# Expert-choice lists in three parts by token range, built partly between the tiles of the output projection

## The reference, cut to what matters

```python
def expert_choice_ffn(h, w_router, w_gate, w_up, w_down):
    t = h.reshape(bsz * n, d)
    cap = max(1, EC_CAPACITY * t.shape[0] // N_EXPERTS)     # 128 of 1024 latents, 32 of 256 context tokens
    aff = jax.nn.softmax((t @ w_router).astype(jnp.float32), axis=-1)
    top_w, top_i = lax.top_k(aff.T, cap)
    xe = t[top_i]
    ...
    out = jnp.zeros_like(t).at[top_i.reshape(-1)].add(ye.reshape(-1, d))
```

## Time and profile before

| | us |
|---|---|
| median of 3 runs | 4786.63 (4785.16 to 4791.69) |
| span of the profiled execution (first to last instruction) | 4782.1 |
| PE busy, share of the span | 4300.4 (90%) |
| VectorE busy, share of the span | 1126.3 (24%) |
| tile loop of the first layer | from 1163.95 to 1340.31 |
| lists of the first layer, from the copy of the rows to the last copy of the merge | from 1341.48 to 1382.22 |

### The profile page before, as it was taken

The page is one execution under the profiler, slowest core; times in us unless marked ns, Lnnn a source line. Parts: engine busy times, 40 slices in busy tenths (PEclk is TensorE's granted clock), DMA queues, the critical chain, the costliest instruction groups (busy, mean ns, idle before and its releaser), DMA issues. The chain is left out here.

```text
span 4782.1 us, 61479 instructions
## 1 busy us (share of the span) xinstructions
PE 4300.4 (90%) x25695; PEld 3548.2 (74%) x25695; DVE 1126.3 (24%) x2316; ACT 1134.9 (24%) x2317; POOL 1134.7 (24%) x1008
## 2 busy tenths in 40 slices
PE   7999999999949999999979998989997699999996
PEld 4677686845549989999967685867454699999996
DVE  2333334411240000001033344333013200001102
ACT  2333333301311111111133333332013111111112
POOL 0605244100112222122214426060001112222221
PEclk7999999999969999999969999999998899999998
DMA  6101111013237667776431111010143467676665
GB/s 228 50 16 40 29 32 38 20 35 132 100 113 242 227 223 242 237 241 232 138 83 36 34 28 50 6 50 6 45 161 123 140 234 239 230 235 223 221 227 183
DMA packets 402928, 618.65 MB, mean 129 GB/s; under 512 B 15110, under 2 KB 167916, under 8 KB 402508
## 3 DMA queue, kind: packets, MB, share of 16 engines
q1 hardware_dynamic: 389980, 571.09, 34.9%
q0 software_dynamic: 12672, 43.26, 3.9%
HBM read 561.88 MB, written 53.48 MB: 129 GB/s over the span
## 5 line engine op out<-in xcount | busy, mean ns | idle before, releaser
L895 PE MATMUL ps<-area,ring 128*128 128x160 f32 x8192 | 1166.1, 306 | 109.2 <-DMA ring<-in_w_up_dram 109.2
L895 PEld LDWEIGHTS ps<-area,ring 128*128 128x128 f32 x8192 | 1151.4, 195 | 122.2 <-issue 120.9
L559 PE MATMUL ps<-ring 128*128 128x512 f32 (+1 forms) x1920 | 715.5, 534 | 50.0 <-issue 26.4
L559 PEld LDWEIGHTS ps<-ring 128*128 128x128 f32 x1920 | 370.3, 195 | 386.8 <-issue 371.3
L522 PE MATMUL ps<-cst,area 128*128 128x128 f32 (+2 forms) x2748 | 402.0, 287 | 236.3 <-DVE area L1423 77.1
L928 PE MATMUL ps<-area,ring 128*128 128x160 f32 x4096 | 597.2, 300 | 0.0
L928 PEld LDWEIGHTS ps<-area,ring 128*128 128x128 f32 x4096 | 562.8, 190 | 4.3
L522 PEld LDWEIGHTS ps<-cst,area 128*128 128x128 f32 (+2 forms) x2748 | 319.9, 147 | 299.1 <-issue 81.8
L1502 POOL TENSOR_TENSOR ring<-ring,condT 128x1024 f32<-128x1024 f32 x128 | 258.4, 2018 | 631.3 <-DMA ring<-in_w_ada_dram 616.3
L1567 POOL DMA_INDIRECT xres<-area,curi x64 | 95.4, 1491 | 1270.7 <-DVE area L1465 1261.0
L1459 DVE TENSOR_TENSOR area<-ps,area 128x160 f32<-128x160 f32 x256 | 83.1, 325 | 1165.7 <-ACT area L1128 1165.7
(11 more groups left out here) (232 smaller groups left out, 4320.8 us busy)
## 6 DMA issues: line engine op xcount, KB each, us to landing
ring<-in_w_gate_dram SPq DMA_DIRECT2D x64, 2048.0 KB, 8.5
ring<-in_w_up_dram SPq DMA_DIRECT2D x64, 2048.0 KB, 14.0
ring<-in_w_down_dram SPq DMA_DIRECT2D x64, 2048.0 KB, 10.1
ring<-in_w_ada_dram SPq DMA_DIRECT2D x64, 512.0 KB, 3.8
area<-xres SPq DMA_DIRECT2D x50, 512.0 KB, 4.1
ring<-in_w_in_dram SPq DMA_DIRECT2D x48, 512.0 KB, 6.1
area<-in_w_ada_dram SPq DMA_DIRECT2D x32, 512.0 KB, 15.0
xres<-area SPq DMA_DIRECT2D x28, 512.0 KB, 2.7
```

The lines of the kernel that those rows point to most:

```text
L559: last = mm(dst[:, a:b], hw[:, j, k, :], hT[:, k, a:b], start=(k == 0), stop=(k == KT - 1))
L895: last = mm(ps[:, at:at + CAP], slot(2 * half + i)[:, k, P * (m % 4):P * (m % 4) + P], xeT[b][:, k, :], start=(k == 0), stop=(k == KT - 1))
```

## The change

The 48 rows are no longer worked together. They become three parts on 16 partitions each: part 0 is the latents of tiles 0 to 3, part 1 those of tiles 4 to 7, part 2 the 256 context tokens. PE turns a part to rows as soon as its affinities exist (`aff_rows`): part 0 in pass 6, part 1 in pass 10, part 2 after pass 11. On VectorE, part 0's 16 rounds stand at the ends of passes 6 to 9, four in each; part 1's rows are taken at the end of pass 10 with 5 rounds, its other 11 rounds follow pass 11, and part 2's 4 rounds, on rows of 256, follow these. The preparation of a padded tile and of the parts' first tokens goes. At the end PE turns six small pieces back instead of two, and VectorE copies them out in two instructions instead of one. The merge is the same.

```diff
+                def aff_rows(part):
+                    pe.wait_ge(aff_ready, (4, 8, T)[part])
+                    if part:
+                        pe.wait_ge(rows_copied, part)
+                    for j in range(PARTS[part] // P):
+                        last = transposes(ps[0:EXPERTS, 7 * BANK + P * j:7 * BANK + P * j + P], affs[:, part, j])
+                    last.then_inc(aff_rows_ps, 1)
...
+                    if i == 6:
+                        aff_rows(0)
+                    if i == T:
+                        aff_rows(1)
+                aff_rows(2)
                 pe.wait_ge(lists_ready, 1)
-                for i, src in enumerate((tv, tf)):
-                    last = transposes(ps[:, LISTS * i:LISTS * i + LISTS], src)
+                for i, src in enumerate((tv[:, 0], turned[:, 0], tv[:, 2], tf[:, 0], turned[:, 1], tf[:, 2])):
+                    n = CAPC if i % 3 == 2 else CAPL
+                    last = transposes(ps[0:n, EXPERTS * i:EXPERTS * i + EXPERTS], src[:, 0:n])
...
-                step(v.memset(affs, -1.0))
-                for at, first in ((0, 0), (32, LHALF), (64, LAT)):
-                    v.memset(first_token[at:min(at + 32, LISTS)], float(first)).then_inc(first_token_set, 1)
+                def take_rows(part):
+                    dve.wait_ge(aff_rows_ps, part + 1)
+                    v.tensor_copy(work[:, 0:PARTS[part]], ps[0:EXPERTS, 7 * BANK:7 * BANK + PARTS[part]]
+                                  ).then_inc(rows_copied, 1)
+                    dve.wait_ge(rows_copied, part + 1)
+                def rounds(part, first, end):
+                    rest = work[:, 0:PARTS[part]]
+                    for r in range(first, end):
+                        q = slice(8 * r, 8 * r + 8)
+                        step(v.max(out=tv[:, part, q], in_=rest))
+                        step(v.max_index(out=ti[:, part, q], in_max=tv[:, part, q], in_values=rest))
+                        if r < ROUNDS[part] - 1:
+                            step(v.match_replace(out=rest, in_to_replace=tv[:, part, q], in_values=rest, imm_value=-1.0))
+                def tokens_of(part):
+                    n = 8 * ROUNDS[part]
+                    step(v.tensor_copy(tf[:, part, 0:n], ti[:, part, 0:n]))
+                    if part:
+                        step(v.tensor_scalar(tf[:, part, 0:n], tf[:, part, 0:n], float(LHALF * part), None, ALU.add))
...
-                dve.wait_ge(aff_rows_ps, 1)
-                step(v.tensor_copy(work, ps[0:LISTS, 7 * BANK:7 * BANK + LHALF]))
-                for r in range(CAPL // 8):
...
+                    if i == 6:
+                        take_rows(0)
+                    if 6 <= i < T:
+                        rounds(0, 4 * (i - 6), 4 * (i - 5))
+                    if i == T:
+                        tokens_of(0)
+                        take_rows(1)
+                        rounds(1, 0, 5)
+                rounds(1, 5, ROUNDS[1])
+                tokens_of(1)
+                step(v.tensor_copy(turned[:, 0], tv[:, 1, ::-1]))
+                step(v.tensor_copy(turned[:, 1], tf[:, 1, ::-1]))
+                take_rows(2)
+                rounds(2, 0, ROUNDS[2])
+                tokens_of(2)
```

More of the change, by code:

```diff
@@ L139, in trunk, with part_lists @@
         wo_end = ring[:, 9216:9728]
[L142 to L152, removed]
+        LHALF = LAT // 2
+        PARTS = (LHALF, LHALF, CTX)
+        ROUNDS = (CAPL // 8, CAPL // 8, CAPC // 8)
+        affs = area[:, 14336:14336 + 4 * 3 * EXPERTS].rearrange("p (q j e) -> p q j e", q=3, j=4)
+        work = area[0:EXPERTS, 14848:14848 + LHALF]
+        def part_lists(at):
+            return area[0:EXPERTS, at:at + 3 * CAPL].rearrange("p (q n) -> p q n", q=3)
+        tv, ti, tf = part_lists(15360), part_lists(15744).bitcast(U32), part_lists(16128)
+        turned = area[0:EXPERTS, 16512:16512 + 2 * CAPL].rearrange("p (q n) -> p q n", q=2)
+        lists = area[:, 16768:16768 + 6 * EXPERTS].rearrange("p (i q e) -> p i q e", i=2, q=3)
+        in_first = area[:, 16896:16896 + EXPERTS]
+        merged = area[:, 16928:16928 + EXPERTS]
         square = area[:, 17664:18688]
@@ L209, in trunk @@
          h2_act, x2_squares, x2_inv_ms, x2_inv_rms, logits_exp, logits_max, mix_added, lists_ready,
-         first_token_set) = shared[0:18]
+         rows_copied) = shared[0:18]
         x2_in = shared[18:20]
@@ L267, in aff_tile @@
         def aff_tile(t):
-            j, at = (t, 0) if t < 4 else (t - 4, 32) if t < LT else (t - LT, 64)
-            return affs[:, j, at:at + EXPERTS]
+            return affs[:, t // 4, t % 4]
         def YF(t):
@@ L1424, in _ @@
                 dve.wait_ge(lists_ps, 1)
-                step(v.tensor_copy(lists, ps[:, 0:2 * LISTS].rearrange("p (i e) -> p i e", i=2)))
+                step(v.tensor_copy(lists[:, :, 0:2], ps[:, 0:6 * EXPERTS].rearrange("p (i q e) -> p i q e", i=2, q=3)[:, :, 0:2]))
+                step(v.tensor_copy(lists[0:CAPC, :, 2], ps[0:CAPC, 0:6 * EXPERTS].rearrange(
+                    "p (i q e) -> p i q e", i=2, q=3)[:, :, 2]))
                 val, idx = lists[:, 0], lists[:, 1]
-                step(v.tensor_tensor(in_first, val[:, 0:EXPERTS], val[:, 32:32 + EXPERTS], ALU.is_ge))
@@ L1429, in _ @@
-                step(v.tensor_copy(merged, idx[:, 32:32 + EXPERTS]))
-                step(v.copy_predicated(merged, in_first.bitcast(I32), idx[:, 0:EXPERTS]))
+                step(v.tensor_tensor(in_first, val[:, 0], val[:, 1], ALU.is_ge))
+                step(v.tensor_copy(merged, idx[:, 1]))
+                step(v.copy_predicated(merged, in_first.bitcast(I32), idx[:, 0]))
                 for j in (0, EXPERTS):
                     w = EXPERTS if j == 0 else 1
-                    v.tensor_tensor(tw[:, 0, j:j + w], val[:, 0:w], val[:, 32:32 + w], ALU.max)
+                    v.tensor_tensor(tw[:, 0, j:j + w], val[:, 0, 0:w], val[:, 1, 0:w], ALU.max)
@@ L1434, in _ @@
                     v.tensor_copy(ix[:, 0, j:j + w], merged[:, 0:w])
-                    v.tensor_copy(tw[0:CAPC, 1, j:j + w], val[0:CAPC, 64:64 + w])
-                    v.tensor_copy(ix[0:CAPC, 1, j:j + w], idx[0:CAPC, 64:64 + w])
+                    v.tensor_copy(tw[0:CAPC, 1, j:j + w], val[0:CAPC, 2, 0:w])
+                    v.tensor_copy(ix[0:CAPC, 1, j:j + w], idx[0:CAPC, 2, 0:w])
                 meet(dve, "dve")
```

## The result

The changed kernel takes 4810.85 us (median of 4 runs, 4803.53 to 4820.79) where the kernel before takes 4785.90 (4784.38 to 4791.69). The ratio over the runs is 1.0048, 95% interval 1.0035 to 1.0061 (the quotient of the two medians is 1.0052). It is slower by half a per cent, as forecast (4814, range 4805 to 4823). A second set of 5 runs gave 4810.12 beside 4789.60, ratio 1.0044 (1.0031 to 1.0057). The profiled execution is one at the low end: 4803.53 us, span 4801.8.

What follows compares the result with a forecast made beforehand. VectorE's list rounds were taken to bound the phase that sets the experts' start. Lists 13.1 us later plus 0.65 behind them give 13.75 per layer, 27.5 in all: from 4786.63 to 4814.1, range 4805 to 4823.

Steps and rivals of the forecast that it cites:

- a round on 16 partitions: VectorE's three list passes on 16 partitions: taken to cost 2.304 us, the same as on 80.
- a round on rows of 256: Part 2's rounds on VectorE: 1.50 us each, bounds 1.15 and 2.30.
- gating of tile 7 late: After pass 6 on VectorE: copy 0.72 plus four rounds 9.22, less the 7.24 of room, 2.70 us late.
- each further tile: Gating of tiles 8 and 9: another 1.98 us late each, four rounds exceeding the room of 7.24.
- modulation of tile 9 late: VectorE in pass 10, behind part 0's last four rounds: 13.36 us later than its former start at 1331.73.
- end of the rounds (the instruction at 1379.89 before) late: First VectorE instruction behind all lists: reached at 1392.98, 13.1 us later than before.
- behind it: six pieces and two copies: After the lists: PE's extra turning 0.5 us and VectorE's second copy 0.15, 0.65 more per layer.
- both waits of pass 10: VectorE's waits of 1.72 before tile 9's modulation and 1.86 for tile 8's logits: both disappear under the rounds.
- Narrow rounds are cheap: Rounds on 16 partitions cost less; below 1.91 us, 17% off, the change wins; at 1.6, 4770.3; chance 0.03.
- The overrun is absorbed: In tiles 7 to 9, faster ACT answers shrink waits of 2.12 and 2.84; 7.8 per layer, 4802.3; chance 0.05.
- Nothing moves: The experts' start hangs on weight loads, so the lists have slack; time stays at 4786; chance 0.04.
- It is worse: Rounds between tiles 10% slower, or PE stalled at tile 8: 8 more per layer, 4830; chance 0.03.

Runs made afterwards that it cites:

- The loop's part: Kernel before plus four extra rounds on an unused scrap row at the ends of passes 6 to 9; 4806.58 us beside 4788.64, ratio 1.0040.
- the tail: Changed kernel without part 0's sixteen rounds, its list left empty; 4789.24 us beside 4788.64 of the kernel before, ratio 1.0001.
- the run with shared rounds: Kernel before, lists kept together, rounds started in pass 10 on the latents' rows, context's rows joining after four; 4773.17 us beside 4788.64, ratio 0.9964.

## Why the prediction was right, step by step

The phase starts 0.10 us later in the profiled execution of the changed kernel (the first tile's gating is at 1177.84, before at 1177.74), which is taken off below.

| step | forecast | measured |
|---|---|---|
| a round on 16 partitions | 2.304 | 2.28 |
| a round on rows of 256 | 1.50 | 1.48 |
| gating of tile 7 late | 2.70 | 2.49 |
| each further tile | 1.98 | 1.78 |
| modulation of tile 9 late | 13.36 | 12.54 |
| logits' maximum of tile 8 late | 11.5 | 10.6 |
| end of the rounds (the instruction at 1379.89 before) late | 13.1 | 11.44 |
| behind it: six pieces and two copies | 0.65 | 0.25 |
| the merge's first instruction late | 13.75 | 11.69 |
| experts' first matmul late | 13.75 | 11.35 |

*The mechanism* held in every step: no idle time between rounds and gating, tile 9's transposes late and tile 8's not, both waits of pass 10 gone, and the second layer like the first (11.35 and 11.44). The loop's part and the tail, run apart, came out at 10.66 and some 1.1 to the merge.

*The sizes* were all a little high. A round is 0.025 us shorter than the value taken, and 34.6 of them stand on the path: 0.9 of the 2.4 us by which the forecast for a layer is too long. The six transposes, for which I took half a us, cost 0.13 more than the two, and with the copies the step behind the lists is 0.4 cheaper than forecast. From the merge to the experts' first matmul it took 14.50 instead of 14.84, which is within the scatter of that piece and nothing that the change does. Most of the rest lies in the boundaries: the first round starts at 1299.71, ahead of the modelled end of the instruction before it (1299.57 + 0.23), where I had put one behind the other, and so does the maximum behind the modulation in pass 10.

*The total* of 24.95 (4810.85 less 4785.90), and 20.5 in the second set, lie on either side of the 22.8 that the two stretches give (23.2 in the second set). The forecast of 27.5 is above all of them. That the time still fell so near to 4814 owes something to chance: the four runs spread over 17 us, for which the range had been widened by 1 us on either side, and the fastest, 4803.53, lies below it. By the stretches alone the time would be 4808.7, also in the range.

*The rivals.* "Narrow rounds are cheap" needed 17% and got 1. "The overrun is absorbed" needed ACT's answers to come earlier; the wait on the square is 2.28 in a late tile (2.12 before) and the one on the square root 2.84 as before. "Nothing moves" is out by the experts' start, which follows the lists in all runs. "It is worse" needed slower rounds between the tiles or a stall of PE at tile 8: the rounds in the gaps take 2.28 as those behind the loop do, and tile 8's transposes are 0.46 later, with no wait ahead of them.

*What I didn't see in advance* is that the rule behind the loss also tells how to win: I weighed the change as work against idle time, and did not ask whether work on more partitions could have been had at no cost.

## What to carry to other kernels

Before moving a step into idle time, ask what it costs where it is: part 0's rounds rode along on other partitions of instructions that had to run anyway, so moving them removed nothing and added their full length. Then lay the moved work against the measured room per gap: three rounds of 2.28 in 7.24 us were free and four were not, since on an engine that runs in order each gap's excess delays the next tile and adds up. What paid was to keep the rounds shared, to start them as soon as the latents' rows were there, and to let the context's rows join later.

## What the runs showed of the hardware

Two executions of the same changed kernel differ by 14.5 us in their spans, 4801.8 and 4816.3, though the changed stretches agree to 0.25. Half of the difference, 7.2, is there before the first tile of the first layer's loop (gating at 1177.84 and 1185.06). In these windows of the two (us, busy time of PE, PEld, DVE, ACT and POOL, granted clock, DMA share, GB/s) the granted clock of one early stretch, a mean between its two levels of 0.5 and 1.0 (1.2 and 2.4 GHz), is lower in the longer execution. First the shorter:

```profile
300.00:600.00 300.00, 280.50 (x1511) 205.16 (x1510) 113.17 (x230) 100.69 (x186) 113.37 (x97) 0.97 0.12 32
```

and the longer:

```profile
300.00:600.00 300.00, 277.71 (x1502) 205.01 (x1501) 115.23 (x230) 99.30 (x190) 106.47 (x91) 0.95 0.11 31
```

What lowers it was not tried, and that it makes the difference is not shown: the run with shared rounds has its first gating at 1183.27, also late, with 0.97 in this window. With a scatter of that size in the rest of the program, a difference of 11 us per layer is better read from the way to the merge or the stretch and only confirmed by the runs.

MAX8 was not wholly free of the number of partitions: 681 ns on 16 and 691 on 80.
